# S5 input in token order, a step-major scratch, early gate weights and a reordered mixing stage in a hybrid decoder step

## The reference

```
hn   = rmsnorm(x, norm_mix_w)
proj = hn @ w_in                       # 1024 -> u 1024 | z 1024 | xbc 1536 | dt 16
# S5: 64 groups of 16 channels, 64 complex states each
h_t  = a * h_(t-1) + b_bar @ u_t       # per group
y    = Re(c @ h_t) + d_skip * u_t
g    = gelu(y);  y_s5 = rmsnorm(g * sigmoid(g @ w_glu))
y_m2 = mamba2(z, xbc, dt)              # gated and normalised
x    = x + concat(y_s5, y_m2) @ w_out
x    = x + peer_ffn(rmsnorm(x))        # product-key experts, gathered rows
```

## Time and profile before

| | us |
|---|---|
| median of 3 runs (4836.53 to 4838.72) | 4837.69 |
| profiled execution, its own time | 4839.17 |
| its span, first to last instruction | 4837.4 |
| project_tokens, to the last store's wait | 0 to 655.6 |
| s5_scan | 655.6 to 939.6 |
| mamba_scan | 939.6 to 1353.0 |
| mix_out | 1353.0 to 1947.4 |
| route_and_experts | 1947.4 to 4837.4 |

### The profile page before, as it was taken

The page is one execution under the profiler, slowest core; times in us unless marked ns, Lnnn a source line. Parts: engine busy times, 40 slices in busy tenths (PEclk is TensorE's granted clock), DMA queues, the critical chain, the costliest instruction groups (busy, mean ns, idle before and its releaser), DMA issues.

```text
span 4837.4 us, 49413 instructions
## 1 busy us (share of the span) xinstructions
PE 2948.8 (61%) x16600; PEld 1442.8 (30%) x16600; DVE 2435.3 (50%) x4868; ACT 1212.1 (25%) x2961; POOL 1326.9 (27%) x1292
## 2 busy tenths in 40 slices
PE   7999962755568577464464554654745645547444
PEld 2255751633344233341131221310411312204110
DVE  1112128157712100457567467576675674765754
ACT  1000010112212100133333333333333333333332
POOL 3000010001100000044444444444444444444443
PEclk9989985566679888675585675765755756657555
DMA  2102151311140101399999999999999999999998
GB/s 93 36 24 73 60 60 22 88 53 33 38 173 0 52 35 43 118 421 421 414 421 421 408 420 418 401 421 407 420 420 400 420 419 407 421 416 405 421 418 364
DMA packets 260355, 1270.67 MB, mean 263 GB/s; under 512 B 49984, under 2 KB 103616, under 8 KB 120128
## 3 DMA queue, kind: packets, MB, share of 16 engines
q0 software_dynamic: 156672, 1140.92, 56.9%
q1 hardware_dynamic: 103392, 126.20, 8.8%
HBM read 1224.97 MB, written 39.69 MB: 261 GB/s over the span
## 4 chain that ended last, share of the span: by engine, by line
DMA 40%; issue 6%; PE 5%; ACT 4%; DVE 4%; POOL 1%; POOLq 0%; SPq 0%; DVEq 0%; ACTq 0%
DMA pe_ring<-in_uv,pe_index_now 39%; PE pe_acc L1792 3%; DVE pe_ring L1715 2%; PE pe_ps_q L1765 1%; PE pe_ps_t L1785 1%; ACT pe_mark L1563 1%; ACT pe_weight L1565 1%; ACT L1563 1%; DVE pe_work_a L1596 1%; POOL pe_ring L1504 1%; ACT L1554 0%; ACT L1537 0%; DVE pe_pos L1648 0%; DVE pe_work_b L1649 0%; ACT pe_x_now L1540 0%
## 5 line engine op out<-in xcount | busy, mean ns | idle before, releaser
L1715 DVE CUSTOM_DVE_ANT_0 pe_ring<-pe_ring,pe_h_rep 128x1024 f32<-128x1024 f32 x1088 | 1329.9, 1226 | 964.1 <-DMA pe_ring<-in_uv,pe_index_now 904.3
L1792 PE MATMUL pe_acc<-pe_ring,pe_weight 128*32 128x256 f32 x8704 | 1023.7, 562 | 1228.5 <-ACT pe_weight L1565 1225.8
L1504 POOL DMA_INDIRECT pe_ring<-in_uv,pe_index_now x1088 | 1195.8, 1099 | 1474.9 <-PE pe_acc L1792 1299.9
L1792 PEld LDWEIGHTS pe_acc<-pe_ring,pe_weight 128*32 128x32 f32 x8704 | 211.5, 131 | 1977.1 <-ACT pe_weight L1565 1919.6
L1563 ACT ACTIVATE pe_mark<-pe_eye,pe_dot 128x32 f32<-128x32 f32 x1088 | 349.4, 321 | 1742.8 <-DVE pe_dot L1715 1740.4
L509 PE MATMUL pj_bank<-pj_x_t,pj_w_buf 128*128 128x512 f32 (+1 forms) x960 | 442.7, 630 | 1.4 <-DVE pj_x_t L396 1.4
L1565 ACT ACTIVATE pe_weight<-pe_mark,pe_gate_now 128x32 f32<-128x32 f32 x1088 | 349.5, 321 | 35.1
L1765 PE MATMUL pe_ps_q<-pe_h_t,pe_w_q 128*128 128x128 f32 x2304 | 329.4, 303 | 1.2 <-ACT pe_h_t L1527 1.2
L1765 PEld LDWEIGHTS pe_ps_q<-pe_h_t,pe_w_q 128*128 128x128 f32 x2304 | 302.8, 213 | 57.6 <-issue 56.0
L509 PEld LDWEIGHTS pj_bank<-pj_x_t,pj_w_buf 128*128 128x128 f32 x960 | 167.8, 199 | 274.1 <-issue 274.1
L220 DVE COPY pj_chan_out<-pj_bank 128x512 f32<-128x512 f32 (+1 forms) x30 | 16.3, 542 | 379.5 <-PE pj_bank L509 379.5
(11 more groups left out here) (297 smaller groups left out, 3194.4 us busy)
## 6 DMA issues: line engine op xcount, KB each, us to landing
pe_ring<-in_uv,pe_index_now POOLq DMA_INDIRECT x1088, 15.9
pj_w_buf<-in_w_in SPq DMA_DIRECT2D x14, 1024.0 KB, 6.1
pe_w_q<-in_w_q SPq DMA_DIRECT2D x4, 2048.0 KB, 18.4
m2s_window<-scratch_xbc SPq DMA_DIRECT2D x8, 786.0 KB, 5.1
scratch_xbc<-pj_chan_out SPq DMA_DIRECT2D x12, 512.0 KB, 2.6
pj_x<-in_x_all SPq DMA_DIRECT2D x9, 512.0 KB, 3.7
scratch_ym<-m2s_y SPq DMA_DIRECT2D x9, 512.0 KB, 2.9
mo_z<-scratch_z SPq DMA_DIRECT2D x9, 512.0 KB, 4.5
```

What stands on the lines that cost most here:

```text
L1504: nc.gpsimd.indirect_dma_start(out=ring[:, p, :], out_offset=None, in_=D["uv"], in_offset=bass.IndirectOffsetOnAxis(ap=row, axis=0)).then_ ...
L1715: V.tensor_tensor_reduce(out=ring[:, p, 0:D_MODEL], in0=ring[:, p, 0:D_MODEL], in1=h_rep[:, g % 2, :], scale=1.0, scalar=0.0, op0=ALU.mult ...
L1792: last = T.matmul(acc[j * PER:(j + 1) * PER, g % 2, 0:COLS], lhs(j), src[:, j * COLS:(j + 1) * COLS], start=first, stop=final)
```

## The change

- The "u" pieces read the tokens in order; the eviction reads PSUM with a stride of eight tokens instead, and a store of a block becomes eight transfers, one per group of 16 channels.
- The scratch between projection and S5, and that between S5 and mixing, are stored as [step, channel, group, chunk]. S5 loads its input in four transfers of 128 partitions and stores its output in four.
- The first "u" unit takes part after part for both blocks, and PE turns tiles 4 to 8 between its pieces.
- The "d" pieces go; dt's 16 columns are made with the last "z" unit (272 columns instead of 256), stored after it.
- In S5 the initial states, a zero and the prompt's states stand in one run of `state`, so that one pair of matmuls of 138 columns takes the place of L692 and L695. The copies into `state` come in two parts.
- `w_glu` is loaded in Mamba's first part, `g_t` in 64 transfers of 16 partitions between Mamba's `load(0)` and its loop, both into SBUF held until mixing.
- In mixing, two PSUM buffers alternate over the tiles; the turn of the next tile stands between the Mamba half and the S5 half (for tile 0 after both).

```diff
         elif n == 0:
+            pieces += [(n, kind, 2 * c + half, part) for part in range(3) for half in range(2)]
...
-    D["u_t"] = nc.dram_tensor("scratch_u_t", (D_MODEL, Q, CHUNKS), F32).ap()
+    D["u_t"] = nc.dram_tensor("scratch_u_t", (Q, S5_CH, S5_GROUPS, CHUNKS), F32).ap()
...
             if kind == "u":
-                return b[:, 0:REST].rearrange("p (s k) -> p s k", s=Q) if part == 2 else b.rearrange("p (s k) -> p s k", s=4)
+                return (b[:, 0:REST] if part == 2 else b).rearrange("p (k s) -> p s k", s=Q)
...
+            if kind == "z" and c == Z_UNITS - 1:
+                copy(dt_out[:, part, :], bank[:, e % 4, CHUNK:CHUNK + HEADS])
...
-                    sp.dma_start(D["u_t"][c * P:(c + 1) * P].rearrange("c s k -> c (s k)"), chan_out[:, use % 2, :]).then_inc(chan_stored[use % 2], 16)
+                    for g in range(P // S5_CH):
+                        sp.dma_start(D["u_t"][:, :, c * (P // S5_CH) + g, :].rearrange("s c k -> c s k"),
+                                     chan_out[g * S5_CH:(g + 1) * S5_CH, use % 2, :].rearrange("c (s k) -> c s k", s=Q)).then_inc(chan_stored[use % 2], 16)
...
-            for i in range(TILES):
+            for i in range(4):
+                turn_tokens(i)
...
-                if e < 3:
-                    pe.wait_ge(t_copied, TILES)
+                if n == 0:
+                    pe.wait_ge(t_copied, (4, 8, 9)[part])
...
-                        if kind == "u":
-                            toks = toks.rearrange("p (k s) -> p s k", s=Q)
-                            toks = toks if part == 2 else toks[:, 4 * part:4 * part + 4, :]
-                        last = T.matmul(source(e, kind, part), lhs, toks, start=first, stop=final)
+                        last = T.matmul(b[:, 0:REST] if part == 2 else b, lhs, toks, start=first, stop=final)
                 last.then_inc((even_done, odd_done)[e % 2], 1)
+                for i in ((4, 5), (6, 7), (8,))[e] if e < 3 else ():
+                    turn_tokens(i)
```

In s5_scan (HALVES goes from 2 to 4):

```diff
             for n in range(HALVES):
-                for s in range(Q):
-                    sp.dma_start(u_t[s * S5_CH:(s + 1) * S5_CH, part(n), :], by_step[s, :, part(n), :]).then_inc(u_in[n], 16)
-            sp.dma_start(rest_start[:, :, :, 0:SEQS], D["s5_h0"]).then_inc(h0_in, 16)
+                sp.dma_start(u_t[:, part(n), :], by_step[:, part(n), :]).then_inc(u_in[n], 16)
+            sp.dma_start(state[:, :, :, 0:SEQS], D["s5_h0"]).then_inc(h0_in, 16)
...
-                for s in range(Q):
-                    sp.dma_start(out_by_step[s, :, groups, :], u_t[s * S5_CH:(s + 1) * S5_CH, groups, :]).then_inc(g_out, 16)
+                sp.dma_start(out_by_step[:, groups, :], u_t[:, groups, :]).then_inc(g_out, 16)
...
-                V.tensor_copy(state[:, r], two(bank[:, r % 4], CHUNKS)).then_inc(v_odd, 1)
+                v = two(bank[:, r % 4], CHUNKS)
+                V.tensor_copy(state[:, r, :, PROMPT:ENDS], v[:, :, SEQS:])
+                V.tensor_copy(state[:, r, :, ENDS:], v[:, :, 0:SEQS]).then_inc(v_odd, 1)
...
+            V.memset(state[:, :, :, SEQS], 0.0).then_inc(scanned, 1)
             dve.wait_ge(h0_in, 16)
-            chain.link(V.memset(rest_start[:, :, :, SEQS], 0.0))
-            V.tensor_copy(rest_start[:, :, :, SEQS + 1], state[:, :, :, SEQS]).then_inc(scanned, 1)
...
-                        T.matmul(y[g][:, CH_REST:], out_w[rows, r, h, S5_CH:], state[rows, r, h, CH_REST - 1:CHUNKS - 1], start=False, stop=False)
-                    for g in range(2):
-                        rows = slice(g * 64, g * 64 + 64)
-                        last = T.matmul(y[g][:, 0:CH_REST], out_w[rows, r, h, S5_CH:], rest_start[rows, r, h, :], start=False, stop=h == 1)
+                        last = T.matmul(y[g], out_w[rows, r, h, S5_CH:], state[rows, r, h, 0:CHUNKS], start=False, stop=h == 1)
```

In mamba_scan and mix_out:

```diff
                 sp.dma_start(start[:], D["ssm_h0"]).then_inc(start_in, 16)
+                sp.dma_start(early["w_glu"][:], D["w_glu"]).then_inc(early_in, 16)
...
                 load(0)
+                for g in range(P // S5_CH):
+                    for c in range(KT):
+                        sp.dma_start(early["g_t"][g * S5_CH:(g + 1) * S5_CH, c],
+                                     D["g_by_step"][:, :, c * (P // S5_CH) + g, :].rearrange("s c k -> c s k")).then_inc(early_in, 16)
                 with sp.Fori(0, MAIN_TILES - 1) as i:
...
-            for c in range(KT):
-                sp.dma_start(g_t[:, c].rearrange("p s k -> p (s k)"), D["g_t"][c * P:(c + 1) * P].rearrange("c s k -> c (s k)")).then_inc(g_in, 16)
-            sp.dma_start(w_glu[:], D["w_glu"]).then_inc(glu_in, 16)
...
+        sums = [ps_out, ps_glu]
...
             for k in range(TILES):
-                if k < MAIN_TILES:
-                    turn(k + 1)
                 pe.wait_ge(m2_t_ready, k + 1)
-                if k:
-                    pe.wait_ge(x_mid_ready, k)
+                if k >= 2:
+                    pe.wait_ge(x_mid_ready, k - 1)
...
                 if k == 0:
                     pe.wait_ge(s5_ready, KT * PARTS)
+                elif k < MAIN_TILES:
+                    turn(k + 1)
...
                 last.then_inc(out_made, 1)
+                if k == 0:
+                    turn(1)
```

More of the change, by code:

```diff
@@ L125, in project_tokens @@
     for n, (kind, c) in enumerate(UNITS):
-        if n == U_UNITS:
-            pieces += [(n, "d", 0, t) for t in range(TILES)]
         if kind == "z":
             pieces += [(n, "z", c, t) for t in range(TILES)]
+        elif n == 0:
+            pieces += [(n, kind, 2 * c + half, part) for part in range(3) for half in range(2)]
         else:
@@ L216, in evict, with stored @@
                 if use >= 2:
-                    eng.wait_ge(chan_stored[use % 2], 16 * (use // 2) + stored_more(use))
+                    eng.wait_ge(chan_stored[use % 2], stored(use))
             if kind == "z" and part < 2 and c:
                 eng.wait_ge(z_stored, 32 * c)
+            if kind == "z" and c == Z_UNITS - 1:
+                copy(dt_out[:, part, :], bank[:, e % 4, CHUNK:CHUNK + HEADS])
             copy(place(kind, c, part), source(e, kind, part)).then_inc(sem_free, 1)
-        def stored_more(use):
-            return 32 * len([v for v in range(use % 2, use, 2) if v >= KT])
+        def stored(use):
+            return 16 * sum(8 if v < KT else 3 for v in range(use % 2, use, 2))
         @block.sync
@@ L266, in store @@
                     sp.dma_start(D["xbc"][:, c, 0:N_META], o[:, SEQ + SAMPLE:SEQ + REST]).then_inc(chan_stored[use % 2], 16)
-                if kind == "d":
+                if kind == "z" and c == Z_UNITS - 1:
                     sp.dma_start(D["dt"].rearrange("(t p) h -> p t h", p=P), dt_out[:]).then_inc(dt_stored, 16)
@@ L499, in _ @@
                     if kind == "z":
-                        last = T.matmul(b[:, 0:CHUNK], x_t[:, k, part * P:(part + 1) * P], w[:, k, :], start=first, stop=final)
-                    elif kind == "d":
-                        last = T.matmul(b[:, 0:HEADS], x_t[:, k, part * P:(part + 1) * P], w_dt[:, k, :], start=first, stop=final)
+                        wide = CHUNK + (HEADS if c == Z_UNITS - 1 else 0)
+                        last = T.matmul(b[:, 0:wide], x_t[:, k, part * P:(part + 1) * P], w[:, k, 0:wide], start=first, stop=final)
                     else:
                         lhs = w[:, k, c % 2 * P:(c % 2 + 1) * P]
-                        toks = x_t[:, k, SEQ:SEQ + REST] if part == 2 else x_t[:, k, part * 512:part * 512 + 512] if kind == "x" else x_t[:, k, 0:SEQ]
-                        if kind == "u":
-                            toks = toks.rearrange("p (k s) -> p s k", s=Q)
-                            toks = toks if part == 2 else toks[:, 4 * part:4 * part + 4, :]
-                        last = T.matmul(source(e, kind, part), lhs, toks, start=first, stop=final)
+                        toks = x_t[:, k, SEQ:SEQ + REST] if part == 2 else x_t[:, k, part * 512:part * 512 + 512]
+                        last = T.matmul(b[:, 0:REST] if part == 2 else b, lhs, toks, start=first, stop=final)
                 last.then_inc((even_done, odd_done)[e % 2], 1)
+                for i in ((4, 5), (6, 7), (8,))[e] if e < 3 else ():
+                    turn_tokens(i)
                 if e == 26 + 16 * (turned // 2) + 4 * (turned % 2) and turned < 8:
@@ L611, in _ @@
                 act.wait_ge(v_made, r + 1)
-                A(state[:, r], two(bank[:, r % 4], CHUNKS), ACT.Copy).then_inc(v_even, 1)
+                v = two(bank[:, r % 4], CHUNKS)
+                A(state[:, r, :, PROMPT:ENDS], v[:, :, SEQS:], ACT.Copy)
+                A(state[:, r, :, ENDS:], v[:, :, 0:SEQS], ACT.Copy).then_inc(v_even, 1)
             act.wait_ge(v_made, PAIRS)
@@ L1150, in mix_out @@
     N = WIDE * Q
-    with ExitStack() as ctx:
+    early = D["early"]
+    with early["held"], ExitStack() as ctx:
         sb = lambda n, s, d=F32: ctx.enter_context(nc.sbuf_tensor("mo_" + n, s, d))
```

(13 more changed lines are left out.)

60 lines of the change are left out of this document (29 added, 31 removed).

## The result

The changed kernel takes 4460.09 us (median, 4455.24 to 4461.69) against 4837.11 for the kernel before: the ratio is 0.9219, with a 95% interval of 0.9203 to 0.9235. Times are medians of fast executions; one execution of the kernel with the mixing order of before was slow, at 6601.17 us, and isn't counted.

What follows compares the result with a forecast made beforehand. Limits differ by stage: PE in projection, load then PE at 1.2 GHz in S5, Mamba's serial loop, mixing's loads and add-to-turn chain. From 4837.7: -158 - 54.5 + 18.5 - 19 - 120.5 = -333.5, giving 4504; 8-in-10 range 4460 to 4555.

Steps and rivals of the forecast that it cites:

- the second of S5: S5's outputs: one matmul of 138 columns for 128 + 10 saves 20% of 97.6 us, -20 (28 at most, 15 at least).
- the rise to 2.4 GHz: Rival, S5's outputs: with the 10-column matmuls gone PE's clock rises, 39 us less, 4465 in all; chance 12%.
- The argument against the rival: S5's outputs: the stage's other matmuls (64 to 138 columns) are as they were, said against the clock rising.
- Projection: Projection: "u" blocks in token order at 15.6 us instead of 31.8, PE ends at 491.0: -158 (134 to 167).
- The startup term: Projection's start: turns, copies and unit 0's pieces, three next to turns at 9.9 us each, end at 77.6 (69.5 to 101).
- The slower rival: Rival, projection: PE stays at 1.2 GHz, the 413 us of work after unit 0 double, 4917 in all; chance 2%.
- S5's load: S5's start: four transfers of 128 partitions replace sixteen, scan starts 23.7 us in, not 53.9: -30 (-28 to -36).
- The last store: S5's end: eight issues of 5.97 us become one, -4.5 (-3 to -6).
- Mamba: Mamba's loop: `load(1)` waits behind the 64 `g_t` transfers, 4.5 MB at 109 GB/s, +18.5 (bounds 0 and 101).
- the prediction's estimate of 38.5 us of delay: Mamba's `load(1)`: by the skill's 0.95 us for 64 KB, 64 `g_t` transfers take 61 us, 4524 in all; not used.
- Mixing: Mixing: first turn earlier without gate loads, -19 (-17 to -21); output tiles at a period of 33 us, -120.5 (-110 to -127.5).
- The price of such a gap: Mixing's output tiles: slowdown of PE after 3 us of idle in mid-tile, 0 to 2.5 us a gap, taken as 1.0.

Runs made afterwards that it cites:

- the mixing order of before: Changed kernel with one PSUM buffer for all tiles and the next tile's turn ahead of the Mamba half again: 4586.08 us, ratio 0.9485.
- The three splits: Changed kernel, S5's state matmul split 128 and 10 (4509.04 us) or 69 and 69 (4511.4 us), or the pair's other matmul split 69 and 69 (4511.4 us).
- the merged kernel: Kernel before with only the single run of `state` and one matmul of 138 columns instead of 128 and 10: 4780.01 us, ratio 0.9881.
- the loads of mixing ahead: Changed kernel with mixing's loads of z and Mamba's result issued ahead of the wait for the add: 4430.42 us, ratio 0.9161.

## Why the prediction was right in most parts and short in its sum

*The step that failed* is the second of S5: the outputs were priced at 1.2 GHz after the change as before, 97.6 x 0.8. The instructions and their shares were right (the first two pairs cost what was summed), but the rise to 2.4 GHz, which stood among the rivals at 12%, took place. Outputs and last store gave back 57.5 us instead of 24.5, so 33 of the 43 us by which the sum fell short of the trace. That the rival's 4465 lies within 5 us of the time is in part luck: it priced the rise at 39 us where it gave 32 (thirty pairs at 1.34 us instead of 2.4), which alone would be 4472; the other parts together gave some 11 more. The three splits and the merged kernel show the cause: in this stage the clock rises with the 6 matmuls of 138 columns to a pair, and stays down with 8 or 10 matmuls that do the same sums, though PE is busy for 98 to 100% in all of them. The splits add loads of weights along with the shorter matmuls, and no run tells these two apart. The argument against the rival, that the other matmuls are as they were, weighed the shapes and not how many short ones stand between them. I also took "busy 98% at 0.50" for a sign that the clock would stay; with PE busy throughout, it was granted at either level. How soon it rises stays open. From the same instructions it took 3.7 to 4.8 us in the changed kernel and four of the experiments, 14.7 in two (the loads of mixing ahead, the mixing order of before; their outputs took 4.5 us longer by it) and 18.3 with the merge alone; it rose in all eight kernels with 6 matmuls, and in none of the four with more.

*Projection* (-165.3 for -158). The strided read is the price, shown by putting it back. The startup term was too high: the pieces between turns took 8.76, 7.03 and 9.80 us, not 9.9 each, at a mean clock of 0.91 over 24 to 60. With the turns behind them they took 35.8 us (24.13 to 59.88) where 29.7 + 14.2 were summed, so "u" ended near 163.5 rather than 171.0 (59.88 + 119.20 less one "x" block of 15.6 in that row). That is inside the bounds given, near the low one. The slower rival, a clock held down through the projection, did not come: x and z ran on at the prices of the earlier trace rows. One reading in the prediction was wrong without harm: the 98 us in the second line of the earlier trace rows are loads of weights; DVE is busy for 45 and ACT for 13 of those 191 us.

*S5's load* (-29.1 for -30): as summed; PE's first matmul came at 5.9 us, all pairs in 18.0. *The last store*: 10.4 us from its first issue to the stage's end before (929.17 to 939.6), 5.0 from the last gelu to that end after (682.75 to 687.74), so 5.4 where 4.5 were summed.

*Mamba* (+20.2 for +18.5). The wait stood where it was expected, and the cause, the queue ahead of `load(1)`, is shown by moving it. The Trainium skill, DMA: Bandwidth & Descriptors, section "Rules for kernel authors", would have small transfers made into one; here 8 instead of 64 changed nothing, and the prediction's estimate of 38.5 us of delay from its section "Measured" was nearly twice the 20.2 that came. The measurement decides: the 4.5 MB in runs of 552 bytes held the queue for 37 us in transfers of 69 KB, and DVE waited as long with transfers of 552 KB.

*Mixing* (-19.5 for -19, and -127.1 for -120.5). The chain from add to turn leaves PE 2.3 to 3.0 us of idle time, as summed. The price of such a gap, taken at 1.0 us, was 0 in four tiles and 1.5 to 1.7 in three: the S5 half takes 13.90 at 1364.23 and 15.43 at 1427.27 after the same idle time. The windows show what differs:

```profile
1363.00:1367.00 4.00, 3.70 (x15) 2.27 (x16) 1.46 (x2) 0.43 (x1) 0.00 (x0) 1.00 0.00 0
1427.00:1431.00 4.00, 4.00 (x9) 1.84 (x8) 1.22 (x1) 0.00 (x0) 0.00 (x0) 0.58 0.00 0
```

In the three costly tiles the clock fell to 0.50 for the first part of the S5 half, in the other four it stayed at 1.00. The length of the gap doesn't decide it: one of 2.26 us was costly, one of 2.98 cost nothing. The seven gaps cost 4.9 us, 2.1 less than summed. Halves follow each other every 13.73 us (1377.96 - 1364.23 by the timeline), where 13.90 was summed, which gives about 2 more; and the turn came 16.3 to 16.9 us after the Mamba half's start, where 0.1 + 16.93 was summed, again about 2. Loading earlier removed the gap. That the gate took 1.9 us longer has no cause shown.

## What to carry to other kernels

Where PE is busy nearly all of a stage and the clock is at its lower level, give the rise of the clock a price and a fair chance when short matmuls are merged: here it brought 32 us beyond the instructions saved. Read each stage's end as a wait: a load put in a loop's queue is paid by whoever waits behind it, and the same load in the stage's first part cost nothing here. When a reordering leaves a small gap on the bounding engine, look along its chain for a load that could have been issued a step earlier.

## What was not expected of the hardware

PE ran for 100 us without a gap at half its clock, with 8 matmuls to a pair (0.50 from 637 to 737), and at full clock with 6 (1.00 from 642 to 681). Records of 69 columns took 0.25 us where those of 138 took 0.32, at the same 1.2 GHz. After idle times of 2.3 to 3.0 us the clock fell to 0.50 for a short while in three cases of seven.
